# Two small constants moved ahead of the large on-chip buffers, and the work blocks padded, in a trunk of two layers

## The reference, cut to what matters

```python
def layer_a(h, g_norm, w_in, conv_w, conv_b, w_r, b_r, w_i, b_i, lam, w_out, mem_k, mem_v):
    proj = rms_norm(h, g_norm) @ w_in
    x_rnn, g_rnn, q_mem, g_mem = jnp.split(proj, [D_RNN, 2 * D_RNN, 2 * D_RNN + D_MEM], axis=-1)
    x_rnn = causal_depthwise_conv(x_rnn, conv_w, conv_b)
    y_rnn = rg_lru(x_rnn, w_r, b_r, w_i, b_i, lam) * jax.nn.silu(g_rnn)
    y_mem = memory_attention(q_mem, mem_k, mem_v) * jax.nn.silu(g_mem)
    return h + jnp.concatenate([y_rnn, y_mem], axis=-1) @ w_out

def layer_b(h, g_norm, w_in, w_out, k_sb, v_sb, mem_k, mem_v):
    proj = rms_norm(h, g_norm) @ w_in
    q_sb, g_sb, q_mem, g_mem = jnp.split(proj, [D_SB, 2 * D_SB, 2 * D_SB + D_MEM], axis=-1)
    y_sb = stick_breaking_attention(q_sb, k_sb, v_sb) * jax.nn.silu(g_sb)
    y_mem = memory_attention(q_mem, mem_k, mem_v) * jax.nn.silu(g_mem)
    return h + jnp.concatenate([y_sb, y_mem], axis=-1) @ w_out
```

## Time and profile before

| | |
|---|---|
| time, median of 3 runs | 1470.63 us (1470.29 to 1471.07) |
| the profiled execution's own time | 1471.48 us |
| its span in the trace | 1469.3 us |
| PE busy | 1460.3 us (99% of the span), 6842 matmuls |
| DVE busy | 998.4 us (68%) |
| ACT busy | 716.3 us (49%) |
| POOL busy | 122.5 us (8%) |
| DMA | 357.97 MB, mean 244 GB/s |
| chain of work that ended last | 99% PE |

### The profile page before, as it was taken

How to read it: one execution, slowest core, us unless ns; L and a number is a source line. 1 busy time by engine, 2 the same in 40 slices (tenths; PEclk the granted TensorE clock), 3 DMA queues, 4 the chain that set the end, 5 groups by cost and what they waited for, 6 DMA issues and landing times.

```text
span 1469.3 us, 18207 instructions
## 1 busy us (share of the span) xinstructions
PE 1460.3 (99%) x6842; PEld 1221.6 (83%) x6842; DVE 998.4 (68%) x1317; ACT 716.3 (49%) x1066; POOL 122.5 (8%) x184
## 2 busy tenths in 40 slices
PE   9999999999999999999999999999999999999998
PEld 7888888888888888888888888888888888888886
DVE  6775568465576896856568676556566566578987
ACT  6764543444544645764325654433333433455465
POOL 0001111111110000000010001111111111100000
PEclk9999999999999999999999999999999999999999
DMA  9877788777795887477999876777887887879863
GB/s 340 293 285 222 159 222 240 194 206 164 195 257 157 316 321 261 161 260 272 343 364 348 302 223 211 245 216 180 243 248 207 221 203 209 242 226 329 314 199 145
DMA packets 154189, 357.97 MB, mean 244 GB/s; under 512 B 7824, under 2 KB 23440, under 8 KB 150032
## 3 DMA queue, kind: packets, MB, share of 16 engines
q1 hardware_dynamic: 103824, 205.98, 40.4%
q0 software_dynamic: 29376, 102.77, 28.6%
q10 hardware_dynamic: 20928, 48.41, 9.1%
HBM read 310.99 MB, written 113.25 MB: 289 GB/s over the span
## 4 chain that ended last, share of the span: by engine, by line
PE 99%; DMA 0%; ACT 0%; SPq 0%; DVE 0%; issue 0%; DVEq 0%; ACTq 0%
PE main L2125 25%; PE main L2126 25%; PE main L2124 25%; PE aux L2124 6%; PE aux L2125 6%; PE aux L2126 6%; PE aux L2482 2%; PE aux L2471 1%; PE aux L2268 0%; DMA f_raw<-in_mem_t 0%; PE main L2176 0%; PE aux L2176 0%; PE main L2197 0%; PE main L2200 0%; PE main L2203 0%; PE aux L2218 0%
## 5 line engine op out<-in xcount | busy, mean ns | idle before, releaser
L2124 PE MATMUL main<-act_hi,w_hi 128*128 128x512 f32 x1216 | 475.5, 391 | 0.0
L2126 PE MATMUL main<-act_hi,w_lo 128*128 128x512 f32 x1216 | 473.7, 390 | 0.0
L2125 PE MATMUL main<-act_lo,w_hi 128*128 128x512 f32 x1216 | 473.5, 389 | 0.0
L2126 PEld LDWEIGHTS main<-act_hi,w_lo 128*128 128x128 f32 x1216 | 228.2, 188 | 47.8
L2125 PEld LDWEIGHTS main<-act_lo,w_hi 128*128 128x128 f32 x1216 | 228.4, 188 | 47.0
L2124 PEld LDWEIGHTS main<-act_hi,w_hi 128*128 128x128 f32 x1216 | 228.3, 188 | 46.8
L1332 DVE SCALAR_TENSOR_TENSOR w_lo<-w_raw,gains,w_hi 128x512 fp32r<-128x512 f32 x180 | 123.3, 747 | 119.6 <-ACT w_hi L702 119.6
L702 ACT ACTIVATE w_hi<-w_raw,gains 128x512 fp32r<-128x512 f32 x180 | 115.4, 713 | 139.4 <-PE main L2126 123.6
L1323 DVE TENSOR_TENSOR w_lo<-w_raw,w_hi 128x1024 fp32r<-128x1024 f32 x88 | 104.2, 1223 | 105.3 <-ACT w_hi L695 105.1
L695 ACT ACTIVATE w_hi<-w_raw 128x1024 fp32r<-128x1024 f32 x88 | 88.5, 1057 | 170.1 <-PE main L2126 126.7
L2124 PE MATMUL main<-w_hi,act_hi 128*128 128x512 f32 (+1 forms) x432 | 163.5, 378 | 0.0
(11 more groups left out here) (321 smaller groups left out, 1863.3 us busy)
## 6 DMA issues: line engine op xcount, KB each, us to landing
w_raw<-in_w_in_a SPq DMA_DIRECT2D x32, 1024.0 KB, 7.1
w_raw<-in_w_in_b SPq DMA_DIRECT2D x32, 1024.0 KB, 7.5
weight_sums<-in_w_out_a POOLq DMA_DIRECT2D x48, 512.0 KB, 7.1
weight_sums<-in_w_out_b POOLq DMA_DIRECT2D x48, 512.0 KB, 7.7
weight_sums<-weight_sums POOLq DMA_DIRECT2D x32, 512.0 KB, 6.7
w_raw<-weight_sums SPq DMA_DIRECT2D x16, 1024.0 KB, 7.5
work<-weight_sums SPq DMA_DIRECT2D x16, 1024.0 KB, 7.8
w_raw<-in_w_mem_kv SPq DMA_DIRECT2D x13, 1024.0 KB, 5.3
```

Source lines behind the costliest of these rows:

```text
L2124: TE.matmul(o, a[0], b[0], start=first, stop=False)
L2125: TE.matmul(o, a[0], b[1], start=False, stop=False)
L2126: return TE.matmul(o, a[1], b[0], start=False, stop=final)
```

## The change

`ident` (512 bytes) and `chan` (384 bytes) are allocated first. All the large buffers move up by these 896 bytes, so that `act_hi` starts at byte 2048 and the others at multiples of 2048. The part of `work` ahead of the blocks is padded by 112 words (448 bytes), so that the blocks start at 512 past a multiple of 2048. The view `xr` keeps its size by a new name, `XW`. The remaining constants move with the end of `work`. Nothing else is edited: no instruction, semaphore, tile size or order.

```diff
+        ident = sb("ident", [P, P])
+        chan = sb("chan", [P, 96])
+        assert nc.sbuf_base % 2048 == 0
         act_hi = sb("act_hi", [P, NK, T], F32R)
...
-        XR = 4 * (T + 4)
+        XW = 4 * (T + 4)
+        XR = XW + 112
...
-        xr = work[:, 0:XR].rearrange("p (b t) -> p b t", b=4)
+        xr = work[:, 0:XW].rearrange("p (b t) -> p b t", b=4)
...
-        ident = sb("ident", [P, P])
         ones = sb("ones", [P, P])
...
-        chan = sb("chan", [P, 96])
```

## The result

| | median | lowest to highest | runs |
|---|---|---|---|
| before | 1470.62 us | 1469.95 to 1473.27 | 22 |
| after | 1468.59 us | 1467.99 to 1471.96 | 22 |

The ratio is 0.9987 with a 95% interval of 0.9981 to 0.9993: 2.03 us less. The forecast was 1469.6 us. The profiled execution of the changed kernel took 1468.66 us.

A forecast was written before the change was run, and what follows sets the result against it. PE's matmul pace was taken as the bound from 16 to 1462 us. The profiled 1471.48 us minus 1.0 for the blocks, other parts zero, gave 1470.5, or 1469.6 us against the median; range 1464.5 to 1475.

The forecast's parts named there:

- First part, the large buffers: 5658 large products, both operands moving from 128 to 0 modulo 512: taken as zero, lower end -74.7 us.
- The argument by translation: Large products: both operands move by the same 896 bytes, so their distance stays 0 modulo 512 and cost is unchanged.
- The argument by the earlier trace: Matmuls of 256 columns at three placements took 283, 284 and 282 ns, so place was taken to cost zero.
- Second part, the blocks: Gates, scores and values go from 64 bytes apart to 0 modulo 512: 1.0 us gain, at most 1.5 us.
- I take two thirds: Of at most 1.5 us from the blocks, 1.0 us was taken, since transposes and the memory branch left doubt.
- All 144 matmuls of the gates, values and scores: 512-column products, 72 gates, 36 values, 36 scores: from 395 to 397 ns down to about 390, 0.9 us together.
- Third to fifth part: ACT and DVE, DMAs, and transposes with `ident` moved: each taken as zero; DMAs -0.4 to 0, transposes 1 us either way.
- The prediction's 0.4 us: First exposed DMA into `f_raw`, 6.67 us: possible gain if alignment made it quicker by one part in 17.
- (a): Rival: nothing moves, not even the blocks' pace, 1470.6 us; chance 0.30.
- (b): Rival: 5658 large products drop from 226.5 towards 213.3 ns, 1396 us, or 1433 for half; chance 0.15.
- the surcharge: The 13.2 ns each 512-column matmul takes beyond 213.3 ns at one column a cycle; 74.7 us over 5658 products.
- (c): Rival: large products fall to the gates' 233 ns as stream and weight load lose step, +36.8 us, 1507 us; chance 0.10.

## Why the prediction was right

**The bound.** PE's stream is the only thing that moved, as the earlier trace rows had it. ACT and DVE kept the durations of the earlier trace rows to 2 ns (1053 and 1051, 1220 and 1220). That the time fell inside the range is no test of the rest: 1464.5 to 1475 us would also have held a kernel in which nothing moved. The tests are the rows and the experiments.

**First part, the large buffers.** Zero was taken, and the constants in front alone gave 0.2 us within an interval of 1.3 either way. The argument by translation (both operands move by the same bytes, so nothing between them changes) is what the experiments confirm, for the two places tried. The argument by the earlier trace rows was weaker than it looked. It compared matmuls of 256 columns, and these answer to the distance in another way than those of 512.

**Second part, the blocks.** The mechanism was right: a distance of 64 bytes made the slow pace. The size was too small by half, 1.0 us against 2.03 (and 1.75 for the padding alone), and both measured gains lie beyond the 1.5 us that this part called the most that could go. Between the profiled executions with the constants alone and after, which both have no stall at the gates, the distances from start to start add up so: gates 0.46 us, `wt,kv` of 512 columns 0.29, the memory branch's values 0.18, scores of 384 and 512 columns 0.15, and slab matmuls 0.69, nearly all of it in the first ten behind a hook. The step that was mis-sized is the deduction "I take two thirds". It rested on the transposes among the hooks and on the memory branch, slow at distance 0, which was read as a sign that the distance may not matter; the padding cured it as well, so it was a sign that a switch of place between neighbours matters too. With it the slab matmuls behind those groups recover, which the sum had counted for gates and stick-breaking attention only: the memory branch's own 0.18 us and 0.15 of the 0.69 were put at nothing. (Two counts were off without moving the sum by more than 0.1 us: two of the nine gates' groups do have a stall in front, and 15 stretches of attention work have slab matmuls behind them, not 12.)

**What stayed slow.** All 144 matmuls of the gates, values and scores were to come down to about 390 ns. 108 did, and so did one pass of the scores. Their 36 have 390, 397 and 397 ns in the three passes, where they had 394, 397 and 397. They come three in a row behind matmuls of 128 and 384 columns, which is fewer than the six or seven that the slab behind gates needed to be quick again. No run tested that this is the reason.

**Third to fifth part.** DMAs: PE's waits for ACT at the start are 0.6 us where the earlier trace rows has 0.8, but they are 0.2 with the constants alone and 0.6 with the padding alone, and the transfer in the chain is another one, of 7.31 us. So the trace shows no gain, and no run isolated one. The prediction's 0.4 us was also read too high from the page that it names: in the Trainium skill, "DMA: Bandwidth & Descriptors", section "How a descriptor splits into AXI transactions", a transaction may be short and the cost is counted in beats of 32 bytes. By that page it is 132 beats instead of 128 for 4096 bytes, 3% of the 6.67 us of the earlier trace rows, an estimate of 0.2 us; no run here shows it. The transposes kept 272 and 273 ns.

**The rivals.** (a), nothing moves, is excluded by the interval (0.9981 to 0.9993). (b), the surcharge is the price of the place, is excluded for the two places compared: the pace is 226.7 ns at 0 and at 1152 past a multiple of 2048 alike. The Trainium skill's 215.7 ns for back-to-back matmuls ("TensorE: Matmul & The Clock Gate", section "Wait — 56ns, not 53.3ns?") was not reached by any 512-column product of this kernel at any distance. (c), slower by losing the step, did not happen since no distance among the large buffers changed. The slower pace that it put the large products at was real: gaps of 16 to 192 bytes between activations and weights cost 17 to 37 us, against its price of 36.8.

## What to carry to other kernels

Where the tensor engine is the bound, compare in the trace the mean duration of matmuls of one width by form. Two paces 6 ns apart at the same width can be a matter of addresses; in this kernel they mostly were. Matmuls that follow narrower ones can be slow for a few in a row at distance 0 too, as the scores were after the change. In long runs of 512-column fp32r matmuls, let the stationary and the moving operands of all neighbours start at the same place modulo 256 bytes. Padding a few words into one buffer does it. Whether that place was 0 or 128 modulo 512 was of no account here; others were not tried for the large products. A buffer added between activations and weights whose size is no multiple of 256 bytes cost this kernel 1.2 to 2.5%, with nothing to see in the profile but PE's own durations.

## What the runs showed of the hardware that I had not expected

- The distance matters modulo 256 bytes: 128 bytes cost 29.6 us, 256 bytes 0.2 (within noise), and 192 bytes act as 64 the other way.
- The projections' matmuls of 256 columns prefer another distance than those of 512 in long runs: 113.4 ns from start to start at 64 bytes, 118.7 at 0.
- One distance can hold both paces: with 16 bytes, stretches of the slabs run at 227 ns and others at 233.
- Half as long a weight load, with half of the output rows, made the matmuls beside it slower, 230.5 ns against 227.6 on average in the slabs.
- The Trainium skill, "SBUF — State Buffer", section "SBUF: two separate sides", gives the tensor engine two independent read ports and says that it never waits on anyone. That is said of waits between engines. Here the place of one of its own operands against the other moved the whole kernel by up to 37 us, with every other engine's instructions unchanged.
